# A hybrid decoder trunk: output norm of the linear attention without GpSimd, with the projection's first unit between the spreads

## The reference

```python
o, s_new = chunk_gated_delta(q, k, v, g, beta, s0)
o = rms_norm(o, out_norm_w) * jax.nn.silu(z.reshape(b, t, GDN_V_HEADS, GDN_DV))
return o.reshape(b, t, GDN_V_DIM) @ w_out, s_new, new_buf
```

## Time and profile before

| | us |
|---|---|
| median of 3 runs | 1568.46 (1565.69 to 1568.99) |
| the profiled execution, its own time | 1565.18 |
| its span, first to last instruction | 1563.5 |
| PE busy | 1461.1 (93% of the span) |
| DVE busy | 943.3 (60%) |
| ACT busy | 796.5 (51%) |
| POOL busy | 333.1 (21%) |
| the output norm, from the barrier to the first product of the projection | 656.1 to 681.0 |

### The profile page before, as it was taken

One profiled execution on the slowest core, in us unless ns is written; L12 is line 12 of the kernel. 1 busy time (PEld: TensorE's weight loads), 2 busy tenths in 40 slices (PEclk: granted clock), 3 DMA queues, 4 the chain that ended last, 5 costly groups with the idle time before them and its releaser, 6 DMA issues. The chain is left out here.

```text
span 1563.5 us, 37037 instructions
## 1 busy us (share of the span) xinstructions
PE 1461.1 (93%) x13462; PEld 1291.8 (83%) x13462; DVE 943.3 (60%) x1812; ACT 796.5 (51%) x1604; POOL 333.1 (21%) x521
## 2 busy tenths in 40 slices
PE   6999989999989999889999999997999989999895
PEld 5999877777767777579999999995766679999895
DVE  5889455555555455574777753535777766777531
ACT  4776744665555556443454442314666654444421
POOL 0334044243354323320000000105233200000000
PEclk7999999999989999979999999998999999999998
DMA  7764373535643443255555665737565545555540
GB/s 172 240 198 154 114 118 60 105 68 107 101 106 78 73 97 75 82 128 141 156 135 154 171 154 117 237 108 237 180 211 186 164 122 136 156 139 159 140 112 34
DMA packets 287842, 211.97 MB, mean 136 GB/s; under 512 B 29711, under 2 KB 279599, under 8 KB 287296
## 3 DMA queue, kind: packets, MB, share of 16 engines
q1 hardware_dynamic: 278454, 178.42, 44.3%
q0 software_dynamic: 9248, 31.80, 7.3%
q10 hardware_dynamic: 42, 0.44, 0.1%
HBM read 187.76 MB, written 22.85 MB: 135 GB/s over the span
## 5 line engine op out<-in xcount | busy, mean ns | idle before, releaser
L621 PE MATMUL psum<-h_rounded,weights_low 128*128 128x320 f32 x1248 | 392.2, 314 | 1.8 <-DVE weights_low L597 1.8
L623 PE MATMUL psum<-h_rounded,weights_high 128*128 128x320 f32 x1248 | 386.7, 310 | 0.0
L622 PE MATMUL psum<-weighted_x_low,weights_high 128*128 128x320 f32 x864 | 266.5, 308 | 0.0
L621 PEld LDWEIGHTS psum<-h_rounded,weights_low 128*128 128x128 f32 x1248 | 235.0, 188 | 7.8 <-DVE weights_low L597 2.5
L623 PEld LDWEIGHTS psum<-h_rounded,weights_high 128*128 128x128 f32 x1248 | 234.7, 188 | 0.0
L597 DVE TENSOR_TENSOR weights_low<-sbuf_resident,weights_high 128x2048 fp32r<-128x2048 f32 x89 | 203.2, 2286 | 28.7 <-ACT weights_high L582 28.6
L582 ACT CAST weights_high<-sbuf_resident 128x2048 fp32r<-128x2048 f32 x90 | 170.0, 1892 | 91.5 <-PE psum L623 58.9
L1285 ACT COPY sbuf_resident<-psum 64x256 f32<-64x256 f32 x256 | 108.5, 424 | 154.6 <-PE psum L1222 152.4
L622 PEld LDWEIGHTS psum<-weighted_x_low,weights_high 128*128 128x128 f32 x864 | 165.3, 191 | 0.2
L699 DVE SCALAR_TENSOR_TENSOR sbuf_stages<-sbuf_stages,sbuf_resident 128x344 f32<-128x344 f32 (+1 forms) x184 | 105.5, 573 | 44.8 <-ACT sbuf_stages L681 41.0
L689 POOL COPY sbuf_stages<-sbuf_stages 128x2 f32<-128x2 f32 (+1 forms) x76 | 34.4, 453 | 454.8 <-DVE sbuf_stages L1998 384.7
(11 more groups left out here) (461 smaller groups left out, 3031.8 us busy)
## 6 DMA issues: line engine op xcount, KB each, us to landing
sbuf_resident<-in_ffn_w_up_dram SPq DMA_DIRECT2D x88, 512.0 KB, 4.9
sbuf_resident<-in_gdn_w_in_dram SPq DMA_DIRECT2D x48, 512.0 KB, 4.8
sbuf_resident<-in_ffn_w_down_dram SPq DMA_DIRECT2D x32, 704.0 KB, 5.8
sbuf_resident<-in_cache_nsa_kv_dram SPq DMA_DIRECT2D x256, 64.0 KB
sbuf_stages<-in_state_gdn_s_dram POOLq DMA_DIRECT2D x16, 512.0 KB, 8.9
out_gdn_s_sample_dram<-sbuf_stages SPq DMA_DIRECT2D x16, 512.0 KB, 4.2
sbuf_resident<-in_gdn_w_out_dram SPq DMA_DIRECT2D x16, 512.0 KB, 5.1
sbuf_stages<-in_cache_nsa_kv_dram POOLq DMA_DIRECT2D x64, 128.0 KB, 2.9
```

The costliest lines, as they stand in the source:

```text
L621: pe.matmul(out, w_lo, x_hi_tile, start=first, stop=False)
L622: pe.matmul(out, w_hi, x_lo_tile, start=False, stop=False)
L623: return pe.matmul(out, w_hi, x_hi_tile, start=False, stop=last)
```

## The change

POOL's part of the norm goes. The squares of pairs 0 and 1, unit 0's low part and all sixteen low parts of tiles are DVE's. DVE makes gate 0 ahead of the inverse and gates 1 to 3 after tiles 3, 7 and 11; unit 0's low part comes after tile 4. ACT casts tiles 0 to 2 ahead of unit 0's weights, and unit 1's weights ahead of tile 10. PE makes spreads 0 to 6, and from there on one tile of unit 0 (three products) after each spread, then the last six tiles. Units 1 to 3 are written out and the loop runs over the rest. The wait on the stored states stays where it was in ACT's list, ahead of the first casts.

```diff
-        POOL_PAIRS, SUM_ORDER, POOL_TILES = (0, 1), (2, 3, 0, 4, 5, 1, 6, 7), (5, 7, 9, 11, 13, 15)
+        DVE_PAIRS, SUM_ORDER = (0, 1), (0, 3, 2, 1, 4, 5, 6, 7)
...
             act.wait_ge(state_out, STATES * QKH + 16)
-            high_part(act, "gdn_out", 0, 0, VH, free=True)
             for j in range(VH):
+                if j == 3:
+                    high_part(act, "gdn_out", 0, 0, VH, free=True)
+                if j == 10:
+                    high_part(act, "gdn_out", 0, 1, VH, free=True)
                 act.wait_ge(S6["dve"].sem, S6["dve"].count(f"out{j}"))
                 act.copy(o_hi[:, j, :], z[:, j, :]).then_inc(x_hi, 1)
-                if j == 11:
-                    high_part(act, "gdn_out", 0, 1, VH, free=True)
...
+            def first_product(k):
+                if k == 0:
+                    pe.wait_ge(lo_done, first_unit + 1)
+                    pe.wait_ge(lane_free[1], free_count("gdn_out", 0, 0, 1))
+                pe.wait_ge(x_lo, SPLITS["gdn_out"][0] + k + 1)
+                return three_products(pe, bank("gdn_out", 0, 1)[:, 0:T], tile(hi, k, 1), tile(lo, k, 1), o_hi[:, k, :], o_lo[:, k, :], k == 0, k == VH - 1)
+            for j in range(VH):
+                spread(j)
+                if j >= 6:
+                    first_product(j - 6)
+            for k in range(VH - 6, VH):
+                last = first_product(k)
+            last.then_inc(unit_done, 1)
...
-        def pool_gate_norm(pool):
...
-            for g in range(3):
-                gated(g)
+            for g in DVE_PAIRS:
+                o = o_heads[:, 2 * g:2 * g + 2, :]
+                dve.tensor_tensor(squares[g], o, o, ALU.mult).then_inc(dve_steps.sem, dve_steps.step(f"sq{g}"))
+            gated(0)
             dve.wait_ge(S6["act"].sem, S6["act"].count("root"))
             dve.reciprocal(inv16, inv16).then_inc(dve_steps.sem, dve_steps.step("inv"))
             for j in range(VH):
                 dve.wait_ge(S6["pe"].sem, S6["pe"].count(f"wide{j}"))
+                if j in (4, 8, 12):
+                    dve.wait_ge(dve_steps.sem, dve_steps.count(f"gated{j // 4}"))
                 dve.tensor_tensor(z[:, j, :], z[:, j, :], psum[:, SPREAD_BANKS[j % 4], 0:T], ALU.mult).then_inc(dve_steps.sem, dve_steps.step(f"out{j}"))
-                if j == 7:
-                    gated(3)
+                if j in (3, 7, 11):
+                    gated(j // 4 + 1)
                 if j >= 2:
                     tile_low(j - 2)
+                if j == 4:
+                    low_part(dve, "gdn_out", 0, VH)
             tile_low(VH - 2)
             tile_low(VH - 1)
-            dve.wait_ge(S6["pool"].sem, S6["pool"].count(f"low{POOL_TILES[-1]}"))
-            dve.memset(xpg[1][:, 0:GP], 0.0).then_inc(x_lo, len(POOL_TILES))
-            dve.wait_ge(lo_done, UNITS["gdn_out"][0] + 1)
             low_part(dve, "gdn_out", 1, VH)
             low_part(dve, "gdn_out", 2, VH)
```

More of the change, by code:

```diff
@@ L633, in multiply_unit @@
                     if from_tile is not None and k >= from_tile and l == lanes[0]:
[L635 to L638, removed]
+                        pe.wait_ge(x_lo, SPLITS[name][0] + k + 1)
                     last = three_products(pe, bank(name, j, l)[:, 0:T], tile(hi, k, l), tile(lo, k, l), high(k), low(k),
@@ L1757, in build @@
         SPREAD_BANKS = (4, 5, 6, 7)
-        POOL_PAIRS, SUM_ORDER, POOL_TILES = (0, 1), (2, 3, 0, 4, 5, 1, 6, 7), (5, 7, 9, 11, 13, 15)
-        ACT_PAIRS = [g for g in SUM_ORDER if g not in POOL_PAIRS]
-        squares = {g: sq6[3 + g] if g in POOL_PAIRS else sq6[ACT_PAIRS.index(g) % 3] for g in SUM_ORDER}
+        DVE_PAIRS, SUM_ORDER = (0, 1), (0, 3, 2, 1, 4, 5, 6, 7)
+        ACT_PAIRS = [g for g in SUM_ORDER if g not in DVE_PAIRS]
+        squares = {g: sq6[3 + g] if g in DVE_PAIRS else sq6[ACT_PAIRS.index(g) % 3] for g in SUM_ORDER}
         S6 = dict(pe=steps("gate_norm_pe", [f"sum{g}" for g in SUM_ORDER] + [f"wide{j}" for j in range(VH)]),
                   act=steps("gate_norm_act", [f"sq{g}" for g in ACT_PAIRS] + ["root"]),
-                  dve=steps("gate_norm_dve", ["pick0", "pick1", "gated0", "gated1", "gated2", "inv"] + [f"out{j}" for j in range(8)] + ["gated3"] + [f"out{j}" for j in range(8, VH)]),
-                  pool=steps("gate_norm_pool", [f"sq{g}" for g in POOL_PAIRS] + [f"low{j}" for j in POOL_TILES]))
+                  dve=steps("gate_norm_dve", ["pick0", "pick1", "sq0", "sq1", "gated0", "inv", "out0", "out1", "out2", "out3", "gated1", "out4", "out5", "out6", "out7",
+                                              "gated2", "out8", "out9", "out10", "out11", "gated3", "out12", "out13", "out14", "out15"]))
         o_hi = rounded("gated_high", o_heads)
@@ L1790, in pe_gate_norm @@
             for g in SUM_ORDER:
-                eng = "pool" if g in POOL_PAIRS else "act"
-                pe.wait_ge(S6[eng].sem, S6[eng].count(f"sq{g}"))
+                squared = S6["dve"] if g in DVE_PAIRS else S6["act"]
+                pe.wait_ge(squared.sem, squared.count(f"sq{g}"))
                 for x in range(2):
@@ L1799, in pe_gate_norm, with spread @@
             pe.wait_ge(S6["dve"].sem, S6["dve"].count("inv"))
-            for j in range(VH):
+            first_unit = UNITS["gdn_out"][0]
+            hi, lo, tile = hi_ring[first_unit % RING], ring_lo[first_unit % RING], single_tile(VH)
+            def spread(j):
                 rows = slice(32 * (j % 4), 32 * (j % 4) + 32)
@@ L1826, in dve_gate_norm @@
             dve.memset(pick_rows[:, 3:4], 1.0).then_inc(dve_steps.sem, dve_steps.step("pick1"))
-            dve.memset(xpg[0][:, 0:GP], 0.0)
+            for xp in xpg:
+                dve.memset(xp[:, 0:GP], 0.0)
             def gated(g):
@@ L1834, in tile_low @@
             def tile_low(j):
-                if j not in POOL_TILES:
-                    dve.wait_ge(x_hi, SPLITS["gdn_out"][0] + j + 1)
-                    dve.tensor_tensor(o_lo[:, j, :], z[:, j, :], o_hi[:, j, :], ALU.subtract).then_inc(x_lo, 1)
-            for g in range(3):
-                gated(g)
+                dve.wait_ge(x_hi, SPLITS["gdn_out"][0] + j + 1)
+                dve.tensor_tensor(o_lo[:, j, :], z[:, j, :], o_hi[:, j, :], ALU.subtract).then_inc(x_lo, 1)
+            for g in DVE_PAIRS:
+                o = o_heads[:, 2 * g:2 * g + 2, :]
+                dve.tensor_tensor(squares[g], o, o, ALU.mult).then_inc(dve_steps.sem, dve_steps.step(f"sq{g}"))
+            gated(0)
             dve.wait_ge(S6["act"].sem, S6["act"].count("root"))
@@ L1862, in pe_add @@
             pe.wait_ge(x_lo, split_count(name) if from_tile is None else SPLITS[name][0] + from_tile)
-            with pe.Fori(0, n // 4) as i:
+            if name == "gdn_out":
+                for j in range(1, 4):
+                    multiply_unit(pe, name, 0, j, single_tile(kn), high, low, kn, lanes=(1,), from_tile=from_tile)
+            with pe.Fori(1 if name == "gdn_out" else 0, n // 4) as i:
                 for j in range(4):
@@ L3217, in _ @@
             pool.wait_ge(stage_closed, 4 * 4)
-            pool_gate_norm(pool)
             pool_core_stored(pool)
```

## The result

The changed kernel takes 1574.3 us (median of 6 runs, 1573.44 to 1577.91), the kernel before, in the same series, 1568.72 us (6 runs): 5.6 us more. The ratio is 1.0038 with a 95% interval of 1.0023 to 1.0054, 3.6 to 8.5 us: slower, by little. The profiled execution took 1575.33 us around a span of 1573.5.

A forecast was written before the change was run, and what follows sets the result against it. PE was taken to set the pace from the first unit's end on. First product at 671.4, nine mixed tiles to 693.5, last products to 698.8 against 690.5: +8.3 us, 1576.8 us on the median, range 1568.5 to 1580.5.

The forecast's parts named there:

- Squares, sums, inverse: Ahead of the first spread: root 0.4 us sooner, inverse ending at 663.45, first spread and first `out` 1.2 us ahead.
- First product: PE's start on unit 0, once DVE has made its low part: 7.0 us of DVE's list, at 671.4.
- The mixed tile: Spread plus three products on PE at half clock: 2.46 us (1.36 + 1.10), nine times, lower bound 1.87.
- The clock in the mix: PE's clock while spreads and products alternate: stays at 0.50 (1.2 GHz) from 671.4 to about 698.
- Rival 2: Clock returns inside the mix after some 5 us; unit 1 starts at 689.1, -1.4 us, 1567 us; chance 0.14.
- The last seven tiles: Unit 0's 21 products without a spread: 5.8 us at half clock, 0.5 taken off, ending at 698.8.
- Rivals 1 and 3: Free division changes, clock down: +3.5 us, 1572, chance 0.10; DVE sets the pace: -4.0 us, 1564.5, chance 0.06.
- rival 3: PE at full clock by 671.4, mixed tile 1.0 us, DVE sets the pace: -4.0 us, 1564.5; chance 0.06.
- The sum: Unit 0's end at 698.8 instead of 690.5: +8.3 us, put on the median as 1576.8 us.
- POOL's lock: POOL making unit 0's low part holds DVE: a tile's low part takes 3.84 us instead of 0.48; gone after the change.

The follow-up runs named there:

- the kernel with the low part on POOL: The changed kernel with all sixteen spreads before unit 0's products again, and unit 0's low part back on POOL; 0.00% against the kernel before.
- the warmed mix: The changed kernel plus matmuls nobody reads where PE is idle, ahead of the inverse and around spreads 4 to 6; +0.15% against the kernel before.

## Why the prediction was right, and where it was off

Slower was forecast with 0.79, 1576.8 us within 1568.5 to 1580.5; it came to 1574.3.

- **Squares, sums, inverse**: forecast 4.7 us from the barrier to the root and 5.2 to the inverse; measured 4.8 and 5.3 (660.24 and 660.80 against 655.47).
- **First product**: forecast 15.3 us, measured 16.0. The list on DVE was as costed, with 2.28 us for unit 0's low part. The miss is at the first spreads: `out0` was put 0.83 us behind the first spread, a figure at full clock, and the clock had fallen by then (0.51 in the first window), so four spreads took 1.45 us instead of 0.82. That is chance of the execution: with the same list up to there, four spreads took 0.82 us in the kernel with the low part on POOL and 1.15 us in the second trace of the changed one.
- **The mixed tile**: forecast 2.46 us, measured 2.46, nine times, and made up as forecast: 1.36 us from spread to product (672.57 to 673.93) and 1.10 from product to spread. Of it the tile without changeovers has 1.86.
- **The clock in the mix**: forecast at 1.2 GHz until about 698; it was there until 699.6. Rival 2 did not occur, and in the warmed mix a clock of 1.00 was lost after 9.6 us.
- **The last seven tiles**: the 0.5 us taken off for an early return of the clock were wrong in the first trace; all 21 products ran at half clock. In the second trace the last six ran at full clock, which is worth 0.6 us:

```profile
696.20 0.33 PE L621 MATMUL psum<-gated_high,weights_low 128*128 128x320 f32 x1
```

- **Rivals 1 and 3** would have needed a tile of 1.87 or about 1.0 us on 32 rows; the spreads over 128 rows reach 1.86 and 0.97, and then DVE does set the pace, as rival 3 has it.
- **The sum**: 8.3 us forecast, 9.4 in the stage and 5.6 or 6.0 in the time. The term for the stage was 1.1 us too small, by the first spreads and the clock's return. That the whole program shows 3 us less than the stage was in no step of the forecast: that the time came out below 1576.8 and not above it was luck, though the stage's own 9.4 us (1578.1) would have been in the range too.
- **POOL's lock**, named as the cause of the 3.84 us stall, was shown. The forecast missed that the two POOL squares held DVE too: in the kernel before the first gate takes 2.47 us beside them, and 1.54 in the changed kernel, which the same lock would explain; no run moves the squares alone. The gain was in the forecast all the same, since it had DVE free before the root ends.

```profile
656.22 2.47 DVE L1831 SCALAR_TENSOR_TENSOR sbuf_stages<-sbuf_stages,sbuf_resident 128x1280 f32<-128x1280 f32 x1
```

## What to carry to other kernels

Filling an engine's waiting time with the next stage's work pays only if the filler does not slow what was there: here spreads that ran four abreast on quarters of the array became serial (at full clock four took 0.82 us side by side; one alone over 128 rows takes 0.53 us, the tile of 0.97 less three products of 0.148), with two changeovers a tile. Price a mix by its own rows: records of the rarer kind alone, the distance at the seams, and the clock at which it will run. If small matmuls must stand between full ones, giving them the full array costs less (0.97 against 1.37 us a tile at full clock), while ahead of the mix the small form is the cheap one.

## What was not expected of the hardware

- The clock fell in the middle of a stretch in which PE's records left no gap: from 1.00 to 0.50 at 684.3, after nearly ten us of 32-row spreads between full products. With the same order on 128 rows it came back within about 5 us of the first product. Between unread full matmuls the same 32-row spreads left it at 1.00 for 11.6 us, so the cause is open.
- The array's changeovers cost 0.60 us a tile at half clock and about 0.40 at full (1.37 - 0.97): not in proportion to the clock.
- Unread matmuls meant to hold the clock did hold it, and cost more than the clock was worth as soon as they stood between matmuls of another size.
